# The gate product of both layers as wide matmuls over two banks by turns

## The chip, the cores and the metric

The kernel runs on one core of a Trainium2 chip. The metric is the device time of one execution in microseconds (us); lower is better. Engines work side by side and are tied by semaphores: PE (TensorE, matrix products), ACT (ScalarE), DVE (VectorE), POOL (GpSimd) and SP, which here issues the transfers of the weights.

## The reference, cut to what matters

Four layers of a network over 256 tokens of width 1024, all in fp32. The first two are other blocks (gated linear attention, stick-breaking attention, both with an MLP) and are not touched. The change is at the end of each of the last two layers:

```
for i in range(DEPTH):                                 # DEPTH = 2
    ...
    h = h + gated_conv_ffn(rms_norm(h, ffn_norm_w[i]), ...)
    gate = jax.nn.sigmoid(rms_norm(h, ple_norm_w[i]) @ w_ple_gate[i])   # 1024 x 1024
    h = h + gate * (p[i] @ w_ple_proj[i])                              # 256 x 1024
return rms_norm(h, final_norm_w)
```

The kernel multiplies by the norm's weight first, takes the product, and applies the one factor per token (the inverse root of the mean square, `rs1`) to the product.

## The kernel before, in words

**Precision and operands.** Every fp32 operand is split into a high and a low part, and a product is high·high + high·low + low·high. Activations lie with the feature on the partitions; `xs` holds for each of 8 feature tiles k the high tokens (`xhi`, 256 columns) and right beside them the low tokens (`xlo`, 256 columns).

**Weight stream.** All weights come as 208 chunks of 128x2048, in the order of use. SP loads chunk c into one of six buffers (`raw`), ACT makes its high part (`split_hi`, the cast of L283), DVE its low part (`split_lo`, the subtraction of L291). There are three buffers for each part, so both wait until chunk c-3 has been used (`chunk_used`), and PE waits for the low part (`lo_made`). A gate product is four chunks, C_GATE[L] to C_GATE[L]+3; chunk j gives 256 output features (two tiles t). Below they are called chunk 0 to 3, the next two (the projection, and the first of the next layer) chunk 4 and 5.

**Two ways to multiply a chunk.** `gemm` (L299 to L301) issues for each of 16 (k, t) three matmuls of 256 columns, all into the same half bank, so that PSUM bank b holds the finished sum for both tiles. `wide_gemm` (L390, L392) issues two: the low weight with the high tokens (256 columns) and the high weight with high and low tokens together (512 columns). It needs two whole banks, b for tile 0 and b+1 for tile 1. In each, columns 0 to 255 (`main_half`) hold two of the terms and columns 256 to 511 (`cross_half`) the third, so that someone has to add the halves. The MLPs and the gated FFN just ahead of the gate product are made so: ACT copies the cross half to SBUF (L1136, L1140), DVE adds the main half to it (L1643, L1668).

**The gate stage before.** PE: `gemm` for chunk j into bank j, j = 0 to 3, no bank used twice; after chunk 1 it sums the squares over the partitions (`squares_sum`, L515) into bank 3, which chunk 3 overwrites later, once `rs_made` says that ACT has read it. Then the projection into `acc` (`ple_projection`). ACT in program order: cast of chunk 2, squares, cast of chunk 3, logarithm and exponential for `rs1` (L981, L982), and then for j = 0 to 3: the cast of chunk j+3 (j = 1 and 2 only), and the sigmoid of output j (L1428) once DVE has scaled it (`z_scaled`). DVE in program order: the subtractions of chunks 1 and 2, the sum of squares (L1548 to L1550), and then for j = 0 to 3: the subtraction of chunk j+3 (j < 3), and the scaling of output j out of PSUM (L2007). After that the products with the projection (L2011), their addition to h (L1864) and, in the first of the two layers, the low part of the next activations (L1541). Every engine takes its instructions strictly in this written order.

Of the kernel before, what the change touches and what calls it, by code (L numbers as in the profile page):

```python
# [6 lines left out]
S = 256  # L7
# [10 lines left out]
LN_EPS, RMS_EPS = 1e-5, 1e-6  # L18
# [16 lines left out]
C_GATE = [c + 3 * N_FF for c in C_FFN]  # L35
# [19 lines left out]
def build_program(nc, xT, xtok, lnp, wstream, wa1, wa2, wf, fbias, pT, params, consts, decay, out):  # L55
    f32, f32r, i32 = mybir.dt.float32, mybir.dt.float32r, mybir.dt.int32
    ALU, ACT = mybir.AluOpType, mybir.ActivationFunctionType
    ctx = ExitStack()
    with ctx:
        def sb(name, shape, dt=f32):  # L60
            return ctx.enter_context(nc.sbuf_tensor(name, shape, dt))

        def sem(name):
            return ctx.enter_context(nc.semaphore(name))
# [11 lines left out]
        kT = sb("kT", [128, NT, S])  # L76
# [39 lines left out]
        def flat(t):  # L116
            return t[:, :, :].rearrange("p t s -> p (t s)")

        yf, sqf, qf, kf, gf, hf = (flat(t) for t in (y, sq, qT, kT, gT, hT))
        wa2_sb = sqf[:, 1536:2048]  # L120
        rs = misc[:, 2048:3072]
        rs1 = misc[:, 2048:2304]
        dec = misc[:, 0:2048].rearrange("p (h s) -> p h s", h=RET_H)

        def wide(ap, n):

            return ap.unsqueeze(1).to_broadcast([ap.shape[0], n, ap.shape[1]])

        def pair(t, j):
            return t[:, 2 * j:2 * j + 2, :]  # L130

        def two(ap):
            return ap.rearrange("p (t s) -> p t s", t=2)


        acc = ctx.enter_context(nc.psum_tensor("acc", [128, NT, S], f32))
        ring = ctx.enter_context(nc.psum_tensor("ring", [128, 4, 512], f32))

        def bank(i):
            return ring[:, i, :]  # L140
# [11 lines left out]
        chunk_used = sem("chunk_used")  # L152
# [21 lines left out]
        z_scaled, gelu_scaled = sem("z_scaled"), sem("gelu_scaled")  # L174
# [10 lines left out]
        signs_made = sem("signs_made")  # L185
        s_z, s_abs, s_ln, s_sp, s_hi, s_L, s_lw, s_w, s_wm, s_o = (sem("sb_" + n) for n in ("z", "abs", "ln", "sp", "hi", "L", "lw", "w", "wm", "o"))
        wf_in = sem("wf_in")
        f_part, f_copied = sem("fox_part"), sem("fox_copied")
        f_log, f_logit, f_ln, f_cum, f_z, f_mx, f_e, f_p, f_td, f_tc, f_o = (
            sem("fox_" + n) for n in ("log", "logit", "lnf", "cum", "z", "mx", "e", "p", "td", "tc", "o"))  # L190
# [79 lines left out]
        def cross_half(b):  # L270

            return ring[:, b:b + 2, 256:512]

        def main_half(b):
            return ring[:, b:b + 2, 0:256]

        def split_hi(act, c, m=0, per=RAW):
            if c >= N_CHUNKS:
                return
            act.wait_ge(raw_in[c % RAW], m * (16 * per // RAW) + 16 * (c // RAW + 1))  # L280
            if c >= SPLIT:
                act.wait_ge(chunk_used, m * per + (c - SPLIT + 1))
            act.copy(whi[:, c % SPLIT, :], raw[:, c % RAW, :]).then_inc(hi_made, 1)  # L283

        def split_lo(dve, c, m=0, per=RAW):
            if c >= N_CHUNKS:
                return
            dve.wait_ge(hi_made, m * per + (c + 1))
            if c >= SPLIT:
                dve.wait_ge(chunk_used, m * per + (c - SPLIT + 1))  # L290
            dve.tensor_tensor(wlo[:, c % SPLIT, :], raw[:, c % RAW, :], whi[:, c % SPLIT, :].bitcast(f32),  # L291
                              ALU.subtract).then_inc(lo_made, 1)
# [3 lines left out]
        def _(pe):  # L296
            def three(o, l1, l2, r1, r2, start, stop, **kw):

                pe.matmul(o, l1, r1, start=start, stop=False, **kw)  # L299
                pe.matmul(o, l1, r2, start=False, stop=False, **kw)  # L300
                return pe.matmul(o, l2, r1, start=False, stop=stop, **kw)  # L301

            def gemm(c, b, x_need=None, m=0, turned=False, between=None):


                pe.wait_ge(lo_made, m * RAW + (c + 1))
                wh, wl = whi[:, c % SPLIT, :], wlo[:, c % SPLIT, :]
                outs = [bank(b)[:, t * 256:t * 256 + 256] for t in range(2)]
                if x_need is not None:

                    for k in range(NT):
                        if turned and k % 4 == 0:
                            pe.wait_ge(x_made, 4 * x_need + k // 2 + 2)
                        if not turned and k % 2 == 0:
                            pe.wait_ge(x_made, 4 * x_need + k // 2 + 1)
                        for t in range(2):
                            w = slice(k * 256 + t * 128, k * 256 + t * 128 + 128)
                            mm = three(outs[t], wh[:, w], wl[:, w], xhi[:, k, :], xlo[:, k, :], k == 0 and t == 0,
                                       k == NT - 1, skip_group_check=True)
                    mm.then_inc(chunk_used, 1)  # L320
                    return
                for t in range(2):
                    if t and between is not None:
                        between()
                    for k in range(NT):
                        w = slice(k * 256 + t * 128, k * 256 + t * 128 + 128)
                        mm = three(outs[t], wh[:, w], wl[:, w], xhi[:, k, :], xlo[:, k, :], k == 0, k == NT - 1)
                mm.then_inc(chunk_used, 1)
# [183 lines left out]
            def squares_sum(n, o):  # L512

                pe.wait_ge(sq_summed, n + 1)
                pe.matmul(o, ones, sq[:, 0, :], start=True, stop=True).then_inc(var_done, 1)  # L515

            def ple_projection(c, L):

                pe.wait_ge(lo_made, c + 1)
                pe.wait_ge(p_lo, L + 1)  # L520
                for j in range(4):
                    pe.wait_ge(y_made, 4 * (2 + 3 * L) + j + 1)
                    for k in range(2):
                        for t in (2 * j, 2 * j + 1):
                            w = slice(k * D + t * 128, k * D + t * 128 + 128)
                            mm = three(acc[:, t, :], whi[:, c % SPLIT, w], wlo[:, c % SPLIT, w], hhi[:, 2, k, :],
                                       hlo[:, 2, k, :], k == 0 and t % 2 == 0, k == 1, skip_group_check=True)
                    mm.then_inc(*((proj_done, 1) if j < 3 else (chunk_used, 1)))
# [299 lines left out]
            for L in range(DEPTH):  # L828
                X = 6 + 4 * L
# [112 lines left out]
                for j in range(4):  # L942
                    if j == 3:
                        pe.wait_ge(rs_made, 3 * L + 3)
                    gemm(C_GATE[L] + j, j, X + 3 if j == 0 else None)
                    if j == 1:
                        squares_sum(3 * L + 2, bank(3)[:, 0:S])
                ple_projection(C_PROJ[L], L)
            for t in range(NT):
                pe.wait_ge(sq_made, 4 * 6 + (t // 2 + 1 if t < 6 else t - 2))  # L950
# [5 lines left out]
        def _(act):  # L956
# [22 lines left out]
            def power(r, psum, scale, eps):  # L979

                own.sync(act.activation(r, psum, ACT.Ln, bias=eps_col[eps], scale=scale))  # L981
                return act.activation(r, r, ACT.Exp, scale=-0.5)  # L982

            def inverse_root(n, psum, eps):

                act.wait_ge(var_done, n + 1)
                power(rs1, psum, 1 / D, eps).then_inc(rs_made, 1)
# [91 lines left out]
            def mlp(n):  # L1079
                c0, free, h0 = C_MLP[n], FREE[f"mlp{n}"], N_UP * n  # L1080

                def crossed(c, i, m=0):
                    act.wait_ge(chunk_used, m * 12 + (c + 1))
                    act.copy(pair(qT, i % 3), cross_half(2 * (i % 2))).then_inc(hid_cross, 1)  # L1084
# [26 lines left out]
                def last_crossed(t):  # L1111
                    act.wait_ge(*((chunk_used, cu + 1) if t else (up_half, n + 1)))
                    act.copy(qT[:, 2 * s + t, :], cross_half(2 * (i % 2))[:, t, :]).then_inc(hid_cross if t else half_cross, 1)
# [210 lines left out]
            for L in range(DEPTH):  # L1324
                X = 6 + 4 * L
# [93 lines left out]
                split_hi(act, C_GATE[L] + AHEAD)  # L1419
                squares_of_h(3 * L + 2)  # L1420
                split_hi(act, C_GATE[L] + 1 + AHEAD)
                inverse_root(3 * L + 2, bank(3)[:, 0:S], RMS_EPS)
                for j in range(4):
                    if 1 <= j < 3:
                        split_hi(act, C_GATE[L] + j + 1 + AHEAD)
                    act.wait_ge(z_scaled, 4 * L + j + 1)
                    z = kf[:, j * 512:j * 512 + 512]
                    act.activation(z, z, ACT.Sigmoid).then_inc(sig_made, 1)  # L1428
# [12 lines left out]
        def _(dve):  # L1441
# [424 lines left out]
            for L in range(DEPTH):  # L1866
                X = 6 + 4 * L
# [133 lines left out]
                for j in range(4):  # L2001
                    if j < 3:
                        split_lo(dve, C_GATE[L] + j + 1 + AHEAD)
                    if j == 0:
                        dve.wait_ge(rs_made, 3 * L + 3)
                    dve.wait_ge(chunk_used, C_GATE[L] + j + 1)
                    dve.tensor_tensor(pair(kT, j), two(bank(j)), wide(rs1, 2), ALU.mult).then_inc(z_scaled, 1)  # L2007
                for j in range(4):
                    dve.wait_ge(*((proj_done, 3 * L + j + 1) if j < 3 else (chunk_used, C_PROJ[L] + 1)))
                    dve.wait_ge(sig_made, 4 * L + j + 1)  # L2010
# [181 lines left out]
```

## Time and the profile before

| | us |
|---|---|
| median of three runs | 1316.61 (1316.28 to 1316.97) |
| the profiled execution, its time | 1316.21 |
| the profiled execution, span from first to last instruction | 1314.5 |
| busy in the span: PE / DVE / ACT | 1297.4 / 927.3 / 671.2 |

A busy PE here is one whose matmuls overlap with their neighbours: a matmul of 256 columns is shown as 0.28 us long while the next starts 0.12 us after it. So the distance from start to start is what a matmul takes of PE's time. All times of rows below are from the start of the span. The gate stage of the first layer (L = 0) begins at 929.14 us, that of the second (L = 1) at 1275.18 us.

### The profile page before, as it was taken

To read this page: it belongs to the slowest core of one execution; us is meant where nothing else is said; L and a number is where in the kernel's file an instruction comes from. 1 tells how busy PE (TensorE), PEld (TensorE's weight loads), DVE (VectorE), ACT (ScalarE), POOL (GpSimd) and SP (SyncE) were. 2 spreads that over 40 slices of the span, in tenths; PEclk is the share of its full clock that TensorE was granted. 3 is DMA by queue.
4 is the path that set the end of the run, shared out by engine and by line. 5 is a ranking of instruction groups with operands and counts; after the bars stand their busy time and mean duration, and the time that the engine had idled before them with its cause. 6 is when DMAs were issued, how large, how long until landed. Compare 5 with 4: busy or idle time off the path is not lost.

```text
span 1314.5 us, 21057 instructions
## 1 busy us (share of the span) xinstructions
PE 1297.4 (99%) x8368; PEld 1155.8 (88%) x8368; DVE 927.3 (71%) x1125; ACT 671.2 (51%) x767; POOL 45.8 (3%) x69
## 2 busy tenths in 40 slices
PE   9999999999999999999999999999999999999998
PEld 8898888887998888887998989999999888999997
DVE  4748655567566766558667787777796769877776
ACT  6645444445565444445444654444655546444454
POOL 0000000000133000001100000000020000000000
PEclk9999999999999999999999999999999999999999
DMA  9634655554433555554554355445545534545520
GB/s 378 263 119 172 245 192 192 191 192 160 161 129 129 217 186 186 186 189 139 186 177 145 129 192 191 179 177 186 192 141 190 191 112 148 219 176 181 188 96 33
DMA packets 34401, 231.85 MB, mean 176 GB/s; under 512 B 4000, under 2 KB 4256, under 8 KB 7200
## 3 DMA queue, kind: packets, MB, share of 16 engines
q1 hardware_dynamic: 31104, 219.17, 46.0%
q10 hardware_dynamic: 3232, 11.76, 2.7%
q8 instruction: 47, 0.77, 0.2%
q14 instruction: 18, 0.15, 0.0%
HBM read 227.77 MB, written 1.05 MB: 174 GB/s over the span
## 4 chain that ended last, share of the span: by engine, by line
PE 85%; DVE 8%; ACT 4%; issue 2%; DMA 1%; DVEq 0%; ACTq 0%
PE ring L392 19%; PE ring L390 10%; PE ring L299 9%; PE ring L301 8%; PE ring L300 8%; PE acc L424 4%; PE acc L426 4%; PE acc L425 4%; PE acc L301 3%; PE acc L299 3%; PE acc L300 3%; DVE wlo L291 3%; ACT whi L283 1%; PE ring L424 1%; PE ring L426 1%
## 5 line engine op out<-in xcount | busy, mean ns | idle before, releaser
L291 DVE TENSOR_TENSOR wlo<-raw,whi 128x2048 fp32r<-128x2048 f32 x206 | 472.3, 2298 | 132.5 <-ACT whi L283 132.0
L283 ACT CAST whi<-raw 128x2048 fp32r<-128x2048 f32 x202 | 384.8, 1908 | 119.7 <-PE ring L301 62.6
L392 PE MATMUL ring<-xs,whi 128*128 128x512 f32 x1184 | 419.6, 398 | 0.0
L390 PE MATMUL ring<-xs,wlo 128*128 128x256 f32 x1184 | 333.4, 282 | 1.1 <-DVE wlo L291 1.1
L392 PEld LDWEIGHTS ring<-xs,whi 128*128 128x128 f32 x1184 | 222.4, 188 | 53.1
L299 PE MATMUL ring<-xs,whi 128*128 128x256 f32 x832 | 240.6, 289 | 1.9 <-DVE xs L1541 0.8
L300 PE MATMUL ring<-xs,whi 128*128 128x256 f32 x832 | 235.3, 283 | 0.0
L301 PE MATMUL ring<-xs,wlo 128*128 128x256 f32 x832 | 235.2, 283 | 0.0
L390 PEld LDWEIGHTS ring<-xs,wlo 128*128 128x128 f32 x1184 | 223.7, 189 | 3.3 <-DVE wlo L291 1.8
L299 PEld LDWEIGHTS ring<-xs,whi 128*128 128x128 f32 x832 | 159.2, 191 | 9.1 <-issue 5.5
L300 PEld LDWEIGHTS ring<-xs,whi 128*128 128x128 f32 x832 | 159.4, 192 | 0.6 <-issue 0.5
L301 PEld LDWEIGHTS ring<-xs,wlo 128*128 128x128 f32 x832 | 159.3, 192 | 0.0
L299 PE MATMUL acc<-hhi,whi 128*128 128x256 f32 x384 | 108.8, 283 | 0.0
L301 PE MATMUL acc<-hhi,wlo 128*128 128x256 f32 x384 | 108.6, 283 | 0.0
L300 PE MATMUL acc<-hlo,whi 128*128 128x256 f32 x384 | 108.6, 283 | 0.0
L424 PE MATMUL acc<-whi,hhi 128*128 128x512 f32 x256 | 100.1, 391 | 0.0
L426 PE MATMUL acc<-whi,hlo 128*128 128x512 f32 x256 | 99.8, 390 | 0.0
L425 PE MATMUL acc<-wlo,hhi 128*128 128x512 f32 x256 | 99.6, 389 | 0.0
L300 PEld LDWEIGHTS acc<-hlo,whi 128*128 128x128 f32 x384 | 73.5, 191 | 0.9
L299 PEld LDWEIGHTS acc<-hhi,whi 128*128 128x128 f32 x384 | 73.5, 191 | 0.4 <-issue 0.4
L301 PEld LDWEIGHTS acc<-hhi,wlo 128*128 128x128 f32 x384 | 73.5, 192 | 0.0
L1084 ACT COPY qT<-ring 128x512 f32<-128x512 f32 x30 | 17.6, 586 | 98.0 <-PE ring L392 95.8
(296 smaller groups left out, 1673.7 us busy)
## 6 DMA issues: line engine op xcount, KB each, us to landing
raw<-wstream SPq DMA_DIRECT2D x206, 1024.0 KB, 4.8
sq<-lnp ACTq DMA_DIRECT2D x3, 1024.0 KB, 4.9
raw<-wstream SPq DMA_DIRECT2D x4, 256.0 KB, 5.2
hT<-xT ACTq DMA_DIRECT2D x4, 256.0 KB, 5.5
raw<-wstream SPq DMA_DIRECT2D x2, 512.0 KB, 8.3
hT<-xtok ACTq DMA_DIRECT2D x1, 1024.0 KB, 18.3
misc<-decay ACTq DMA_DIRECT2D x1, 1024.0 KB, 4.7
kT<-lnp ACTq DMA_DIRECT2D x1, 1024.0 KB, 4.8
```

Source lines behind the costliest of these rows:

```text
L283: act.copy(whi[:, c % SPLIT, :], raw[:, c % RAW, :]).then_inc(hi_made, 1)
L291: dve.tensor_tensor(wlo[:, c % SPLIT, :], raw[:, c % RAW, :], whi[:, c % SPLIT, :].bitcast(f32), ALU.subtract).then_inc(lo_made, 1)
L299: pe.matmul(o, l1, r1, start=start, stop=False, **kw)
L300: pe.matmul(o, l1, r2, start=False, stop=False, **kw)
L301: return pe.matmul(o, l2, r1, start=False, stop=stop, **kw)
L390: pe.matmul(bank(b + t)[:, 0:256], wl[:, w], xhi[:, k, :], start=k == 0, stop=False, skip_group_check=True)
L392: mm = pe.matmul(bank(b + t), wh[:, w], xs[:, k, :, :].rearrange("p a s -> p (a s)"), start=False, stop=k == NT - 1, skip_group_check=True)
L424: pe.matmul(o, l1[:, k, at], wh[:, w], start=first and k == 0, stop=False, skip_group_check=True)
L425: pe.matmul(o, l1[:, k, at], wl[:, w], start=False, stop=False, skip_group_check=True)
L426: mm = pe.matmul(o, l2[:, k, at], wh[:, w], start=False, stop=last and k == 1, skip_group_check=True)
L1084: act.copy(pair(qT, i % 3), cross_half(2 * (i % 2))).then_inc(hid_cross, 1)
```

## The change

PE uses `wide_gemm` for the four gate chunks, into the bank pairs 0-1, 2-3, 0-1, 2-3. ACT copies the cross half of each into an SBUF buffer (`z_part`, two by turns), DVE adds it to the main half, writes the sum to `kT` (`z_sum`), and scales that in a second instruction, from SBUF. Chunks 2 and 3 wait on PE until the sum of the chunk two before has been taken. The squares are summed into `acc` tile 7 in place of bank 3.

```diff
+        def z_part(j):
+            return two(gf[:, (j % 2) * 512:(j % 2) * 512 + 512])
@@ tensor
                 for j in range(4):
                     if j == 3:
                         pe.wait_ge(rs_made, 3 * L + 3)
-                    gemm(C_GATE[L] + j, j, X + 3 if j == 0 else None)
+                    if j >= 2:
+                        pe.wait_ge(z_sum, 4 * L + j - 1)
+                    wide_gemm(C_GATE[L] + j, 2 * (j % 2), X + 3 if j == 0 else None)
                     if j == 1:
-                        squares_sum(3 * L + 2, bank(3)[:, 0:S])
+                        squares_sum(3 * L + 2, acc[:, 7, :])
@@ scalar
                 split_hi(act, C_GATE[L] + 1 + AHEAD)
-                inverse_root(3 * L + 2, bank(3)[:, 0:S], RMS_EPS)
+                def z_crossed(j):
+                    act.wait_ge(chunk_used, C_GATE[L] + j + 1)
+                    act.copy(z_part(j), cross_half(2 * (j % 2))).then_inc(z_cross, 1)
+                z_crossed(0)
+                inverse_root(3 * L + 2, acc[:, 7, :], RMS_EPS)
                 for j in range(4):
                     if 1 <= j < 3:
                         split_hi(act, C_GATE[L] + j + 1 + AHEAD)
+                    if j < 3:
+                        z_crossed(j + 1)
                     act.wait_ge(z_scaled, 4 * L + j + 1)
                     z = kf[:, j * 512:j * 512 + 512]
                     act.activation(z, z, ACT.Sigmoid).then_inc(sig_made, 1)
@@ vector
                     if j < 3:
                         split_lo(dve, C_GATE[L] + j + 1 + AHEAD)
+                    dve.wait_ge(z_cross, 4 * L + j + 1)
+                    dve.tensor_tensor(pair(kT, j), main_half(2 * (j % 2)), z_part(j), ALU.add).then_inc(z_sum, 1)
                     if j == 0:
                         dve.wait_ge(rs_made, 3 * L + 3)
-                    dve.wait_ge(chunk_used, C_GATE[L] + j + 1)
-                    dve.tensor_tensor(pair(kT, j), two(bank(j)), wide(rs1, 2), ALU.mult).then_inc(z_scaled, 1)
+                    dve.wait_ge(z_sum, 4 * L + j + 1)
+                    dve.tensor_tensor(pair(kT, j), pair(kT, j), wide(rs1, 2), ALU.mult).then_inc(z_scaled, 1)
```

## Rows read from the trace of the kernel before

**Rows 1.** The page: busy time of the engines, and PE's granted clock in 40 slices.
```profile
PE 1297.4 (99%) x8368; PEld 1155.8 (88%) x8368; DVE 927.3 (71%) x1125; ACT 671.2 (51%) x767; POOL 45.8 (3%) x69
...
PEclk9999999999999999999999999999999999999999
```
**Rows 2.** PE in order of time (start us, us, engine, line), from FFN to next layer.
```profile
906.31 0.28 PE L390 MATMUL ring<-xs,wlo 128*128 128x256 f32 x1
...
917.62 0.28 PE L299 MATMUL acc<-hhi,whi 128*128 128x256 f32 x1
...
929.14 0.28 PE L299 MATMUL ring<-xs,whi 128*128 128x256 f32 x1
...
940.67 0.60 PE L515 MATMUL ring<-sq,cst 128*128 128x256 f32 x2
940.92 0.47 PE L299 MATMUL ring<-xs,whi 128*128 128x256 f32 x1
...
952.61 0.28 PE L299 MATMUL acc<-hhi,whi 128*128 128x256 f32 x1
...
960.48 0.39 PE L299 MATMUL ring<-xs,whi 128*128 128x256 f32 x1 [0.35 <-DVE xs L1541]
960.70 0.28 PE L300 MATMUL ring<-xs,whi 128*128 128x256 f32 x1
```
**Rows 3.** The chain that ended last (start us, us, what), in and behind the first gate stage.
```profile
951.39 1.46 DVE wlo L291
...
959.55 0.87 DVE xs L1541 x2
```
**Rows 4.** DVE in order of time, gate stage of the first layer.
```profile
939.43 2.28 DVE L291 TENSOR_TENSOR wlo<-raw,whi 128x2048 fp32r<-128x2048 f32 x1
942.27 0.69 DVE L2007 TENSOR_TENSOR kT<-ring,misc 128x512 f32<-128x512 f32 x1 [0.55 <-ACT misc L982]
946.00 2.29 DVE L291 TENSOR_TENSOR wlo<-raw,whi 128x2048 fp32r<-128x2048 f32 x1 [3.04 <-ACT whi L283]
948.21 0.68 DVE L2007 TENSOR_TENSOR kT<-ring,misc 128x512 f32<-128x512 f32 x1
...
953.60 1.28 DVE L2007 TENSOR_TENSOR kT<-ring,misc 128x512 f32<-128x512 f32 x2
954.80 0.68 DVE L2011 TENSOR_TENSOR kT<-kT,acc 128x512 f32<-128x512 f32 x1
955.51 0.69 DVE L1864 TENSOR_TENSOR hT<-hT,kT 128x512 f32<-128x512 f32 x1
956.12 0.68 DVE L2011 TENSOR_TENSOR kT<-kT,acc 128x512 f32<-128x512 f32 x1
```
**Rows 5.** ACT in order of time, gate stage of the first layer.
```profile
942.25 1.28 ACT L1428 ACT_TABLE_LOAD   x1
943.55 0.63 ACT L1428 ACTIVATE kT<-kT 128x512 f32<-128x512 f32 x1
944.09 1.89 ACT L283 CAST whi<-raw 128x2048 fp32r<-128x2048 f32 x1
```
**Rows 6.** ACT and DVE in order of time: one FFN chunk's halves joined and scaled.
```profile
912.16 0.59 ACT L1136 COPY y<-ring 128x512 f32<-128x512 f32 x1 [3.74 <-PE ring L392]
...
912.78 0.69 DVE L1643 TENSOR_TENSOR y<-ring,y 128x512 f32<-128x512 f32 x1 [2.04 <-ACT y L1136]
...
913.51 0.69 DVE L1646 TENSOR_TENSOR qT<-y,misc 128x512 f32<-128x512 f32 x1
```
**Rows 7.** PE in order of time, second layer: start of the projection.
```profile
1298.64 0.28 PE L299 MATMUL acc<-hhi,whi 128*128 128x256 f32 x1
```
**Rows 8.** DVE in order of time, second layer.
```profile
1300.28 0.69 DVE L2011 TENSOR_TENSOR kT<-kT,acc 128x512 f32<-128x512 f32 x1 [0.75 <-PE acc L301]
...
1304.60 0.69 DVE L2011 TENSOR_TENSOR kT<-kT,acc 128x512 f32<-128x512 f32 x1
```
**Rows 9.** Who PE waited for, whole span: us in total, times, longest.
```profile
PE ring L367 <- DVE y L1718: 1.3, 1, 1.3
```

More of the change, by code:

```diff
@@ L187, in build_program @@
         wf_in = sem("wf_in")
+        z_cross, z_sum = sem("z_cross"), sem("z_sum")
         f_part, f_copied = sem("fox_part"), sem("fox_copied")
```

## The prediction

> **What bounds the kernel now.** I read the page first. PE is busy 1297.4 of 1314.5 us, and DVE and ACT are far from full [rows 1]. So the span is PE's work, and a change pays by taking matmul time away or costs by making PE, or whoever hands to it at a seam, late. Next I read PE in order of time through the gate stage. From 929.14, chunks 0 and 1 run until 940.67, then the squares, then chunks 2 and 3 from 940.92 until the projection starts at 952.61, and nothing in it is a wait [rows 2]. Before the change PE never waits in this stage. That doesn't mean that only PE is tight there: the chain that ended last runs through DVE's and ACT's part of the stage [rows 3], because DVE then makes the activations for which PE waits in the next layer (0.35 us before 960.48, [rows 2]). So two lines run abreast: PE's, and the one of casts, subtractions, scalings and sigmoids, which ends in the products with the projection (954.80, [rows 4]). Both have to be carried through the change. The second layer repeats the first 346.03 us later (PE at 1298.64 against 952.61) [rows 2, 7], up to its end.
>
> **Part 1: the matmuls.** A chunk of `gemm` is 48 matmuls. From 929.14 to 940.67 there are two chunks, so one takes 5.765 us, 0.120 a matmul. A wide chunk has 32 matmuls; two of them in the FFN run from 906.31 to 917.62 without a gap, so one takes 5.655 us [rows 2]. The array streams the same 768 columns for each (k, t) either way, so only the cost of an instruction is saved: 0.11 us a chunk, 0.22 before the squares, 0.88 over eight chunks. That is all that the change can win, 0.07%.
>
> [...]
>
> **Part 2: the first bank wait.** Chunk 2 now goes into chunk 0's banks, and waits for the sum of output 0. PE is ready for it at 940.67 - 0.22 + 0.25 (the squares) = 940.70. ACT copies the cross half of chunk 0 right behind the cast of chunk 3, in a stretch in which it stood idle, so it isn't late. DVE is: the sum stands in its queue behind the subtraction of chunk 3, which starts at 939.43, because the subtractions of chunks 1 and 2 and the sum of squares fill DVE before it. This subtraction's successor starts 2.21 us after it (948.21 after 946.00) [rows 4], so the sum starts at 941.64. It is like L1643, which takes 0.69 [rows 6], so it ends at 942.33, and PE starts 0.06 later (960.42, where the activations of L1541 end, to 960.48, [rows 2, 3]), at 942.39. PE stands 1.69 us. Before, DVE scaled output 0 at 942.27 and nobody waited for it; the same lateness was free, since the banks weren't reused.
>
> **Part 3: the sigmoid of output 0 and the second bank wait.** The squares come 0.22 us earlier, so ACT is through with the exponential at about 942.03 instead of 942.25. Now the copy of chunk 1's cross half follows (0.59, [rows 6]), and only then the table load of the sigmoid: 942.03 + 0.61 = 942.64. The sigmoid starts 1.30 after the start of its table load [rows 5], at 943.94 against 943.55, 0.39 late; DVE's scaling is done by 943.05, so the table is the last to come. Behind the sigmoid in ACT's queue is the cast of chunk 4 (944.09, now 944.48), and behind that cast waits DVE's subtraction of chunk 4 (946.00, now 946.39). Only behind this stands the sum of output 1: 948.21 + 0.39 = 948.60, end 949.29. PE needs it for chunk 3. Chunk 2 started at 942.39 and runs 5.655, with 0.10 more because the first matmul after a stand is followed at 0.22 instead of 0.12 (960.48 to 960.70) [rows 2]; it is over at 948.15. PE starts chunk 3 at 949.35, and stands 1.20 us. The projection starts at 949.35 + 5.75 = 955.10 instead of 952.61, 2.49 late. Here the change's wait sits in a loop: chunk 3 waits for a sum that stands behind a subtraction that stands behind a cast that stands behind a sigmoid.
>
> **Part 4: the line through DVE, first layer.** Each output now costs DVE a sum and a scaling. The scaling waits for the sum's own semaphore, so it starts 0.71 after it (as 955.51 after 954.80); the next instruction without such a wait starts 0.61 later (956.12 after 955.51) [rows 4]. Scaling 1: 948.60 + 0.71 = 949.31, against 948.21, so 1.10 late. Sigmoid 1, the cast and the subtraction of chunk 5 hang on it and are 1.10 late too (there was no slack there, [rows 3]), and the sum of output 2 starts at 953.60 + 1.10 = 954.70. Its scaling 955.41. The sum of output 3 could start at 956.02; its copy starts when chunk 3's last matmul has ended, 955.10 + 0.16 = 955.26, and hands over 0.62 later (912.16 to 912.78, [rows 6]), at 955.9, just in time. Scaling 3 at 956.73, first product at 957.34 against 954.80: 2.54 late. From there the work is as before, all on DVE, and PE's next layer hangs on it [rows 2], so layer one gives 2.54.
>
> **Part 5: second layer.** The PE side is the same: first stand 1.69, second 1.20, projection at 1301.13 for 1298.64. There is no chunk 5, so DVE is free when chunk 3 ends at 1301.29. The copy and hand-over take 0.03 + 0.62, the sum starts at 1301.94, the scaling at 1302.65, the first product at 1303.26, against 1300.28: 2.98 late. But before, the products followed the projection, 1.44 apart (1300.28 to 1304.60 for three) [rows 8], while DVE alone needs 1.32 (954.80 to 956.12) [rows 4]. So it catches up 0.36: the fourth starts at 1303.26 + 3.96 = 1307.22 against 1304.60, 2.62 late. The projection's own last part allows 1307.09, so DVE decides by a hair. The final norm follows as before.
>
> **What costs nothing.** Moving the squares to `acc` tile 7: its last reader, the addition at L1864, is over before chunk 0 is half done. The eight copies on ACT, 0.59 each: the first and the last three fall where ACT waited for DVE or PE; the one of chunk 1 is priced above. The weight stream isn't touched, and its loads only get 2.5 us more time.
>
> **The sum.** 2.54 + 2.62 = 5.2 us. On the profiled execution that is 1316.21 + 5.2 = 1321.4 (span 1319.7); the median of the runs is 0.4 above that execution, so 1321.8, 0.39% slower.
>
> **The rivals.** *The second wait closes.* If ACT and DVE reached the sum of output 1 before PE asked (1.2 us earlier than I work out), only the first stand of 1.69 less the matmuls saved would be left, about 1.4 a layer on PE's line; the second layer's tail adds its 0.4 to 0.6. The DVE line must then be shorter too. That gives +3.2, 1319.8. The sigmoid table's 0.39 speaks against it, with the queue order. Chance 8 in 100. *PE doesn't stand* (the other side). Then the whole effect is the 0.88 of part 1, 1315.8, not slower. Its place is the sum of output 0: it decides from the point at which this sum ends by 940.64. It would have to stand ahead of the 2.21 us of the subtraction, and the written order forbids that. What is left is a trace whose distances mislead, or a seam elsewhere that swallows both delays. PE waits for DVE right behind the first layer's stage [rows 2], which speaks against slack there, and behind the second there is only the tail. Chance 6, of which 3 with one layer's delay swallowed (+2.6, 1319.2). *A table load more.* The copies stand between exponential and sigmoid and between sigmoids. If one asked for another table, each pair of switches would cost 1.28 to 2.6 us [rows 5] a layer, 1324 to 1327. The casts between the sigmoids bring no load now, and are the same operation. Chance 3. *PE's clock falls.* The granted clock is full in all slices [rows 1], past a wait of 1.3 us near the start [rows 9]. The new stands are 1.7 and 1.2 us, in one stage. [...] Chance 3. [...]
>
> **How the numbers follow.** My forecast has 80 in 100. What it can't know: the sum reading two banks with a stride (as L1643, which does just that), the restart after a stand (0 to 0.3 a stand, four of them), a wide chunk's time in this stage (between the FFN's 5.655 and `gemm`'s 5.765, up to +0.9), and which of two nearly equal lines ends last; together about -1.0 to +1.5. Range 1319.5 to 1323.6: it takes in the closed second wait and a small part of the table case. Changes under 0.2% (2.6 us) can hardly be told from none. Slower 0.91 (forecast, closed second wait, table, clock, less the part of these that ends under +2.6), the same 0.07, faster 0.02.
>
> **What would show it.** In the profile of the changed kernel: PE idle ahead of L390 by DVE's sum, twice a layer, about 1.7 and 1.2 us, four waits and some 5.8 us in all; L390 and L392 128 more each, L299 to L301 128 fewer each; the sigmoid's table load 0.39 later against the stage's start; first product at DVE 28.2 us after the stage's start (957.34 - 929.14), in the second layer 28.1; the clock still full. The prediction is wrong if PE shows no wait at chunk 3, or if the next layer's start takes back some of the first 2.5 us.

## The result and the profile after

The changed kernel takes 1321.42 us (median of 7 runs, 1320.78 to 1321.81) against 1316.71 (7 runs beside them): 1.0037 times as long, 95% interval 1.0028 to 1.0046. That is 4.7 us slower; 1321.8 was forecast, with a range of 1319.5 to 1323.6. The profiled execution has a span of 1319.7 us.

The page of the changed kernel, busy time, granted clock, and the two groups of the wide pair among the costliest:

```profile
PE 1298.0 (98%) x8240; PEld 1148.9 (87%) x8240; DVE 932.3 (71%) x1133; ACT 675.2 (51%) x775; POOL 45.7 (3%) x69
...
PEclk9999999999999999999999999999999999999999
...
L397 PE MATMUL ring<-xs,whi 128*128 128x512 f32 x1312 | 464.9, 397 | 0.0
L395 PE MATMUL ring<-xs,wlo 128*128 128x256 f32 x1312 | 370.0, 282 | 5.7 <-DVE kT L2020 2.4
```

PE's busy time is what it was [rows 1], and the span is 5.2 us longer: the loss is not work, it is standing. The granted clock is full in every slice, 0.999 of full speed over the execution, as in the kernel before, so that rival is out. The wide pair has 128 more each (1312 for 1184), and the idle time ahead of its first matmul is now 5.7 us, where it was 1.1. The same line of the page of the kernel before:

```profile
L390 PE MATMUL ring<-xs,wlo 128*128 128x256 f32 x1184 | 333.4, 282 | 1.1 <-DVE wlo L291 1.1
```

Who PE waited for in the changed kernel (us in total, times, longest). L395 is the first matmul of a wide pair, L2020 the new sum:

```profile
PE ring L395 <- DVE kT L2020: 2.4, 2, 1.2
PE ring L395 <- issue: 2.3, 2, 1.2
...
PE ring L372 <- DVE y L1733: 1.3, 1, 1.3
PE ring L395 <- DVE wlo L296: 1.1, 2, 0.5
```

Four new waits, two in each layer. The trace ties two of them to the sum, and calls the other two "issue", that is without a releaser that it can name; the order of time shows what they are. PE in the first gate stage, the lines that answer to [rows 2]:

```profile
934.98 0.39 PE L395 MATMUL ring<-xs,wlo 128*128 128x256 f32 x1
...
940.74 0.59 PE L520 MATMUL acc<-sq,cst 128*128 128x256 f32 x2
942.54 0.38 PE L395 MATMUL ring<-xs,wlo 128*128 128x256 f32 x1 [1.21 <-DVE kT L2020]
...
947.85 0.28 PE L395 MATMUL ring<-xs,wlo 128*128 128x256 f32 x1
949.53 0.36 PE L395 MATMUL ring<-xs,wlo 128*128 128x256 f32 x1 [1.17 <-issue]
```

And DVE beside it, the lines that answer to [rows 4]; L296 is the subtraction, L2020 the sum, L2024 the scaling, L2028 the product with the projection:

```profile
939.60 2.29 DVE L296 TENSOR_TENSOR wlo<-raw,whi 128x2048 fp32r<-128x2048 f32 x1
941.80 0.68 DVE L2020 TENSOR_TENSOR kT<-ring,gT 128x512 f32<-128x512 f32 x1
942.59 0.69 DVE L2024 TENSOR_TENSOR kT<-kT,misc 128x512 f32<-128x512 f32 x1
946.54 2.29 DVE L296 TENSOR_TENSOR wlo<-raw,whi 128x2048 fp32r<-128x2048 f32 x1 [3.26 <-ACT whi L288]
948.75 0.68 DVE L2020 TENSOR_TENSOR kT<-ring,gT 128x512 f32<-128x512 f32 x1
949.47 0.69 DVE L2024 TENSOR_TENSOR kT<-kT,misc 128x512 f32<-128x512 f32 x1
...
954.86 0.68 DVE L2020 TENSOR_TENSOR kT<-ring,gT 128x512 f32<-128x512 f32 x1
...
957.52 0.68 DVE L2028 TENSOR_TENSOR kT<-kT,acc 128x512 f32<-128x512 f32 x1
```

The first sum ends at 942.48, and PE resumes 0.06 later. The second ends at 949.43, and PE resumes 0.10 later: that "issue" is the same wait. Both sums stand right behind a subtraction of 2.3 us. The stage begins at 929.30 here, so DVE's first product comes 957.52 - 929.30 = 28.22 us into it, against 954.80 - 929.14 = 25.66 before [rows 2, 4]: 2.56 late.

### The profile page after: what moved, and what is told of

Its sections match the earlier page's. It is cut to its first block, busy times and chain, and to the rows that moved or that the text cites. A ratio compares the mean times of both kernels' runs of the same rounds, so it can differ in the third digit from the quotient of the medians.

```text
span 1319.7 us, 20819 instructions
## 1 busy us (share of the span) xinstructions
PE 1298.0 (98%) x8240; PEld 1148.9 (87%) x8240; DVE 932.3 (71%) x1133; ACT 675.2 (51%) x775; POOL 45.7 (3%) x69
## 4 chain that ended last, share of the span: by engine, by line
PE 84%; DVE 9%; ACT 4%; issue 2%; DMA 1%; DVEq 0%; ACTq 0%
PE ring L397 20%; PE ring L395 10%; PE ring L304 8%; PE ring L306 7%; PE ring L305 7%; PE acc L429 4%; PE acc L431 4%; PE acc L430 4%; PE acc L306 3%; PE acc L304 3%; PE acc L305 3%; DVE wlo L296 3%; ACT whi L288 2%; PE ring L429 1%; PE ring L431 1%
## 5 line engine op out<-in xcount | busy, mean ns | idle before, releaser
L296 DVE TENSOR_TENSOR wlo<-raw,whi 128x2048 fp32r<-128x2048 f32 x206 | 472.3, 2298 | 132.5 <-ACT whi L288 132.0
L397 PE MATMUL ring<-xs,whi 128*128 128x512 f32 x1312 | 464.9, 397 | 0.0
L395 PE MATMUL ring<-xs,wlo 128*128 128x256 f32 x1312 | 370.0, 282 | 5.7 <-DVE kT L2020 2.4
L397 PEld LDWEIGHTS ring<-xs,whi 128*128 128x128 f32 x1312 | 246.4, 188 | 58.4
L395 PEld LDWEIGHTS ring<-xs,wlo 128*128 128x128 f32 x1312 | 247.9, 189 | 9.9 <-DVE kT L2020 3.2
L304 PE MATMUL ring<-xs,whi 128*128 128x256 f32 x704 | 204.0, 290 | 1.9 <-DVE xs L1556 0.8
L305 PE MATMUL ring<-xs,whi 128*128 128x256 f32 x704 | 199.1, 283 | 0.0
L304 PEld LDWEIGHTS ring<-xs,whi 128*128 128x128 f32 x704 | 134.7, 191 | 9.0 <-issue 5.7
L305 PEld LDWEIGHTS ring<-xs,whi 128*128 128x128 f32 x704 | 134.8, 192 | 0.6 <-issue 0.5
```

The source lines that it names most:

```text
L395: pe.matmul(bank(b + t)[:, 0:256], wl[:, w], xhi[:, k, :], start=k == 0, stop=False, skip_group_check=True)
L397: mm = pe.matmul(bank(b + t), wh[:, w], xs[:, k, :, :].rearrange("p a s -> p (a s)"), start=False, stop=k == NT - 1, skip_group_check=True)
```

## The experiments

Every kernel was timed beside the kernel before. Runs of one kernel lie up to 2 us apart (the kernel before from 1315.59 to 1317.08, the free banks from 1317.98 to 1320.03), so beside the medians stand four distances in each trace, which leave out what happened ahead of the first gate stage. They are differences of starts in the order of time: from the start of the first gate stage (first matmul of chunk 0) to DVE's first product; from the same start to that of the second gate stage, which holds the whole effect on layer one; from the second stage's start to DVE's fourth product; and from there to the end of the span, which holds the effect on layer two. The second distance runs through the whole next layer and is less exact than the first: in the eight traces of the experiments it reads 0.1 to 0.2 more against before than the first product does, and what makes that isn't shown.

| kernel | us, median | ratio (95%) | 1st product, layer 1 | stage 1 to stage 2 | 4th product, layer 2 | stage 2 to end |
|---|---|---|---|---|---|---|
| before | 1316.71 | | 25.66 | 346.04 | 29.42 | 39.3 |
| changed | 1321.42 | 1.0037 (1.0028 to 1.0046) | 28.22 | 348.60 | 32.08 | 41.8 |
| free banks | 1319.07 | 1.0020 (1.0011 to 1.0029) | 28.23 | 348.74 | 29.31 | 39.1 |
| matmuls alone | 1316.35 | 0.9997 (0.9988 to 1.0006) | 25.54 | 346.15 | 29.13 | 39.1 |
| sums, narrow | 1319.42 | 1.0021 (1.0012 to 1.0030) | 28.31 | 348.84 | 29.60 | 39.3 |
| copy behind cast | 1320.50 | 1.0032 (1.0020 to 1.0045) | 27.74 | 348.28 | 31.61 | 41.3 |
| sums first | 1317.18 | 1.0005 (0.9996 to 1.0014) | 26.77 | 347.28 | 29.30 | 39.0 |
| best order | 1315.88 | 0.9997 (0.9988 to 1.0006) | 25.32 | 345.79 | 29.30 | 39.0 |
| best order again | 1315.48 | 0.9993 (0.9984 to 1.0002) | 25.33 | 345.84 | 29.08 | 38.7 |
| last chunk narrow | 1315.66 | 0.9993 (0.9984 to 1.0002) | 24.91 | 345.51 | 29.12 | 39.0 |

(The kernel before ran again beside each group: 1316.68 beside the free banks, the matmuls, the narrow sums and the sums first; 1316.10 beside the moved copy and the best order; 1316.39 beside the last two.)

The theory is the prediction's: two lines run abreast, PE's through the bank waits, and that of DVE and ACT through the sums, the late sigmoid and the subtractions; both are late by about the same. The chief rival is the plain reading of the profile after, that PE's stands are the cost.

**1. Free banks.** Chunks 2 and 3 go into the accumulator's four banks, which are empty then, and the projection into the ring. PE waits for the sums of outputs 0 and 1 only ahead of the projection.

```diff
-                    if j >= 2:
-                        pe.wait_ge(z_sum, 4 * L + j - 1)
-                    wide_gemm(C_GATE[L] + j, 2 * (j % 2), X + 3 if j == 0 else None)
+                    wide_gemm(C_GATE[L] + j, 2 * (j % 2), X + 3 if j == 0 else None, to=acc_bank if j >= 2 else bank)
...
+                pe.wait_ge(z_sum, 4 * L + 2)
                 ple_projection(C_PROJ[L], L)
...
-                    act.copy(z_part(j), cross_half(2 * (j % 2))).then_inc(z_cross, 1)
+                    act.copy(z_part(j), z_cross_half(j)).then_inc(z_cross, 1)
```

> The changed kernel without bank reuse: chunks 2 and 3 go into the four accumulator banks, the projection into the ring, so PE has no wait for a sum. Two-lines theory (PE's line and the DVE/ACT line are both late, about equally): PE's two stands per layer vanish, but DVE's first product in layer one stays 2.5 us late, because sums, scalings and the late sigmoid are still in its queue; only layer two, which ends on PE's projection, gets its delay back (about -0.3 against before). Time about +2.3 over before, 1319.0. Rival (the stands of PE are the whole cost): all of it comes back, 1315.8 to 1316.2. Rival (wide matmuls are slow here): nothing comes back, 1321.

Measured 1319.07. The largest of PE's waits in this kernel (L310 is `gemm`, L1562 the low part of its activations):

```profile
PE ring L310 <- DVE xs L1562: 3.6, 3, 2.8
```

PE in order of time, the longest of these three waits, at the start of the next layer:

```profile
960.40 0.35 PE L310 MATMUL ring<-xs,whi 128*128 128x256 f32 x1 [2.81 <-DVE xs L1562]
```

The stands inside the gate stage are gone: squares at 11.44 and projection at 23.18 us into the stage, 0.3 earlier than before. In layer one that buys nothing: the first product is where the changed kernel has it (28.23 to 28.22), and PE stands 2.81 us at the start of the next layer instead. In layer two, where the rest waits for the end of chunk 3 on PE, all comes back at the fourth product. So about half of the loss would stay if the banks were never reused, and the chief rival falls. In the profile after, PE's waits of 2.4 and 2.3 us add up to nearly the whole loss, and still they alone don't make it in layer one.

**2. The matmuls alone.** The layout of 1, without copies and sums. DVE scales the main half, so the third term of the product is left out.

```diff
-                    dve.wait_ge(z_cross, 4 * L + j + 1)
-                    dve.tensor_tensor(pair(kT, j), z_main_half(j), z_part(j), ALU.add).then_inc(z_sum, 1)
-                    dve.wait_ge(z_sum, 4 * L + j + 1)
-                    dve.tensor_tensor(pair(kT, j), pair(kT, j), wide(rs1, 2), ALU.mult).then_inc(z_scaled, 1)
+                    dve.wait_ge(chunk_used, C_GATE[L] + j + 1)
+                    dve.tensor_tensor(pair(kT, j), z_main_half(j), wide(rs1, 2), ALU.mult).then_inc(z_scaled, 1)
```

> The wide matmuls alone, in the same banks as e1, with no copy and no sum: DVE scales the main half only, so the third term of the product is left out. Two-lines theory: two chunks take 11.44 us as in the changed kernel (chunk 1 waits for its low part), the squares come 0.1 early; layer one gains 0.1 (DVE's line decides), layer two 0.4 (PE's line): 1316.2. Rival (a wide chunk in this stage costs more than gemm's): above 1316.7. Rival (all 0.88 of the saving is on the path): 1315.8.

Measured 1316.35, not to be told from no change. The first product is 0.12 earlier, the fourth of layer two 0.29. The wide form isn't slower here; it saves a tenth of a microsecond a chunk in layer two and two tenths in layer one (see the last section), and most of that isn't on the path.

**3. The sums alone.** The narrow matmuls into four banks, with the copies and sums where the change has them; copy and sum both read the finished bank, so the gate's input is doubled.

```diff
-                    if j >= 2:
-                        pe.wait_ge(z_sum, 4 * L + j - 1)
-                    wide_gemm(C_GATE[L] + j, 2 * (j % 2), X + 3 if j == 0 else None)
+                    gemm(C_GATE[L] + j, j, X + 3 if j == 0 else None)
...
-                    act.copy(z_part(j), cross_half(2 * (j % 2))).then_inc(z_cross, 1)
+                    act.copy(z_part(j), two(bank(j))).then_inc(z_cross, 1)
...
-                    dve.tensor_tensor(pair(kT, j), main_half(2 * (j % 2)), z_part(j), ALU.add).then_inc(z_sum, 1)
+                    dve.tensor_tensor(pair(kT, j), two(bank(j)), z_part(j), ALU.add).then_inc(z_sum, 1)
```

> The other half of the change alone: gemm's narrow matmuls into four banks as before, but with ACT's four copies and DVE's four sums in the places where the change has them (copy and sum read the finished bank, so the gate's input is doubled). PE waits for no sum. Two-lines theory: layer one about +2.75 at the first product (sigmoid 0.58 late with no matmul time saved, then a sum ahead of scaling 1, a sum ahead of scaling 3), layer two about +0.2: together +2.9, 1319.6. Rival (only PE's stands cost): within 0.3 of before.

Measured 1319.42. First product 28.31, 2.65 late; fourth product of layer two 0.18 late. Without one wait of PE in the gate stage and without wide matmuls, eight copies and eight sums cost 2.7 us in these places of two queues (6 shows that it is the places). Together with 1 this says where the loss sits: layer one's half in DVE's and ACT's line, layer two's half in PE's bank waits. In layer one PE's line is late beside it, but by less: its projection starts 25.96 us into the changed kernel's stage, and the first product follows a projection by 1.64 where nothing else holds it (1298.64 to 1300.28, [rows 7, 8]). By this estimate PE alone would hold it to 27.60, 1.9 late and not 2.56. No run keeps PE's waits and frees DVE's line, so this part isn't tested by itself.

**4. One copy moved.** ACT copies chunk 1's cross half behind the cast of chunk 4 instead of ahead of the sigmoid's table load.

```diff
                     if 1 <= j < 3:
                         split_hi(act, C_GATE[L] + j + 1 + AHEAD)
-                    if j < 3:
+                    if j == 1:
+                        z_crossed(1)
+                    if 1 <= j < 3:
                         z_crossed(j + 1)
```

> The changed kernel with one of ACT's copies moved: that of chunk 1 from ahead of the sigmoid's table load to behind the cast of chunk 4. Nothing else. Two-lines theory: it takes the copy's 0.58 us out of the way of sigmoid 0, the cast and the subtraction of chunk 4, the sum of output 1 and so of both lines, in both layers: -0.6 each, 1320.2; PE's second stand shrinks from 1.2 to 0.6, the first stays. Rival (the second stand hangs on something other than that queue): no change, 1321.4.

Measured 1320.50. First product 0.48 earlier than in the changed kernel, fourth product of layer two 0.47 earlier, and the second stands together 1.3 us where they were 2.3, while the first keep their 2.4. The distances alone show this: the second stage starts 0.32 earlier and the tail is 0.5 shorter, but against the kernel before beside it (1316.10) the time is 4.4 longer, which can't be told from the changed kernel's 4.7. The term was 0.1 too large. The changed kernel's ACT (L989 the exponential, L1432 the copy, L1443 the sigmoid) shows why:

```profile
941.88 0.42 ACT L989 ACTIVATE misc<-misc 128x256 f32<-128x256 f32 x1
942.20 0.57 ACT L1432 COPY gT<-ring 128x512 f32<-128x512 f32 x1
942.78 1.28 ACT L1443 ACT_TABLE_LOAD   x1
944.08 0.63 ACT L1443 ACTIVATE kT<-kT 128x512 f32<-128x512 f32 x1
```

The copy starts 0.10 before the exponential has ended, so it costs the table load 0.48 and not 0.58. The whole chain of copy, table, sigmoid, cast, subtraction, sum and PE moved by that 0.48: one copy on ACT decides when PE starts chunk 3.

**5. The sums first.** DVE's order changed only: the sum of output 0 ahead of the subtraction of chunk 3, each next sum behind the scaling before it. The banks are reused as in the change.

```diff
+                summed(0)
                 for j in range(4):
                     if j < 3:
                         split_lo(dve, C_GATE[L] + j + 1 + AHEAD)
-                    dve.wait_ge(z_cross, 4 * L + j + 1)
-                    dve.tensor_tensor(pair(kT, j), main_half(2 * (j % 2)), z_part(j), ALU.add).then_inc(z_sum, 1)
...
                     dve.tensor_tensor(pair(kT, j), pair(kT, j), wide(rs1, 2), ALU.mult).then_inc(z_scaled, 1)
+                    if j < 3:
+                        summed(j + 1)
```

> The changed kernel with DVE's order changed: the sum of output 0 ahead of the subtraction of chunk 3, and each next sum directly behind the scaling before it, ahead of the next subtraction. Banks are reused as in the change. Two-lines theory: both stands of PE go, because only the order made them; the late sigmoid (0.37) stays, the sum and scaling of output 3 stay behind the last subtraction: first product of layer one 1.1 late, layer two -0.3, together +0.8, 1317.5. Rival (reusing two banks by turns is itself the cost): stands remain, 1320 to 1321.

Measured 1317.18. No stand is left in the gate stage (projection 22.96 and 23.18 us in), with the same two bank pairs by turns. The first product is 1.11 late, as expected, though the median can't be told from before. So reusing two pairs of banks costs nothing in itself; the place of the sum in DVE's queue did.

**6. The best order, twice.** Besides, on ACT the cast of chunk 4 ahead of sigmoid 0 and that of chunk 5 ahead of sigmoid 1, on DVE sum and scaling of output 2 ahead of the subtraction of chunk 5.

```diff
-                    if 1 <= j < 3:
-                        split_hi(act, C_GATE[L] + j + 1 + AHEAD)
                     if j < 3:
                         z_crossed(j + 1)
+                    if j < 2:
+                        split_hi(act, C_GATE[L] + j + 2 + AHEAD)
                     act.wait_ge(z_scaled, 4 * L + j + 1)
...
+                    if j in (0, 1, 3):
+                        split_lo(dve, C_GATE[L] + (2 if j == 3 else j) + 1 + AHEAD)
...
+                    if j == 3:
+                        summed(3)
...
+                    if j < 2:
+                        summed(j + 1)
```

> The sums first, and besides on ACT the cast of chunk 4 ahead of sigmoid 0 and that of chunk 5 ahead of sigmoid 1, on DVE sum and scaling of output 2 ahead of the subtraction of chunk 5. All parts of the change are kept. Two-lines theory: nothing is late any more; layer one ends 0.4 earlier than before, bound by chunk 3's end, its copy, sum and scaling; layer two 0.3 earlier: 1316.0. Rival (the sums cannot be hidden, DVE is too full): 1317 or more.

> The best order once more, beside the kernel above on the same chip: -0.5 against before by the distances of its first trace, 1316.1 where before is 1316.7.

Measured 1315.88 and 1315.48, beside 1316.10 and 1316.39. DVE in the first gate stage of the first of them (L2019 the sum, L2030 the scaling, L2036 the product; the stage starts at 929.48):

```profile
939.77 0.68 DVE L2019 TENSOR_TENSOR kT<-ring,gT 128x512 f32<-128x512 f32 x1
940.37 2.28 DVE L296 TENSOR_TENSOR wlo<-raw,whi 128x2048 fp32r<-128x2048 f32 x1
942.57 0.68 DVE L2030 TENSOR_TENSOR kT<-kT,misc 128x512 f32<-128x512 f32 x1
943.17 0.69 DVE L2019 TENSOR_TENSOR kT<-ring,gT 128x512 f32<-128x512 f32 x1
944.78 2.29 DVE L296 TENSOR_TENSOR wlo<-raw,whi 128x2048 fp32r<-128x2048 f32 x1 [0.92 <-ACT whi L288]
...
953.47 0.69 DVE L2019 TENSOR_TENSOR kT<-ring,gT 128x512 f32<-128x512 f32 x1 [1.56 <-ACT gT L1432]
954.19 0.69 DVE L2030 TENSOR_TENSOR kT<-kT,misc 128x512 f32<-128x512 f32 x1
954.80 0.68 DVE L2036 TENSOR_TENSOR kT<-kT,acc 128x512 f32<-128x512 f32 x1
```

All of the change's work is in it, and the whole loss of 4.7 us is gone. What is left in front of the first product is the copy of chunk 3 and its sum and scaling.

**7. The last chunk narrow.** As 6, with chunk 3 by `gemm` into bank 2 and scaled straight out of it.

```diff
-                    wide_gemm(C_GATE[L] + j, 2 * (j % 2), X + 3 if j == 0 else None)
+                    if j == 3:
+                        gemm(C_GATE[L] + 3, 2)
+                    else:
+                        wide_gemm(C_GATE[L] + j, 2 * (j % 2), X + 3 if j == 0 else None)
...
+                    if j == 3:
+                        dve.wait_ge(chunk_used, C_GATE[L] + 4)
+                        dve.tensor_tensor(pair(kT, j), two(bank(2)), wide(rs1, 2), ALU.mult).then_inc(z_scaled, 1)
+                        continue
```

> The best order, with chunk 3 multiplied by gemm's narrow matmuls into one bank and scaled straight out of it, so that only chunks 0 to 2 are wide and have a sum. Two-lines theory: in the best order the first product (25.32 us after the stage's start) is held by chunk 3's copy, sum and scaling alone; without copy and sum it comes when the projection's first part is done, at 24.9 against 25.66 before, so layer one gains 0.75 and layer two, which ends on PE's projection, 0.2: together -0.9 to -1.0, 1315.7 where before is 1316.7. Rival (the best order is at PE's bound already, and chunk 3's 0.1 us of matmuls is lost): same as or 0.1 above the best order's -0.5.

Measured 1315.66. The first product comes at 24.91, where the projection allows it, 0.75 earlier than before. But the second stage starts only 0.53 earlier, and the median can't be told from that of 6. The step is shown in the trace; that it is worth more than 6 is not.

## Why the prediction was right

**Size.** 5.2 us were forecast on the span; the profiled spans differ by 5.2 (1319.7 to 1314.5) and the stage distances by 2.56 + 2.5 = 5.1. The medians differ by 4.7, so the forecast was 0.5 high, inside the interval (3.7 to 6.1 us). That the spans agree to the tenth is in part luck: 0.16 of the difference lies ahead of the first gate stage (929.30 to 929.14), and the profiled execution of the kernel before, 1316.21, is quicker than all seven runs beside the changed kernel.

**Part 1, the matmuls:** right for the wide pair, mis-sized for what it brings before the squares. Two chunks were to take 11.31 us; they take 11.44, so 0.09 is saved and not 0.22. The sum left out that chunk 1 has to wait for its own low part: that subtraction starts at 932.64, ends at 934.93, and PE starts chunk 1 at 934.98, 5.68 us after chunk 0. The wait itself costs 0.03, and the slow restart of the first matmul (the next starts 0.22 after it, at 935.20) another 0.10. Before, the low part came 0.14 ahead of need (932.48 + 2.28 against 934.90) and didn't show. A gain on PE ran into the next engine's date within one chunk. Part 3 begins with the opposite slip: the copy was to cost the sigmoid 0.61 and costs 0.48 (experiment 4). The two slips cancel, and that is luck; the sigmoid is 0.37 late where 0.39 was forecast. Experiment 2 puts the saving at 0.10 us a chunk (chunks 2 and 3 with the squares 11.74 us in layer two, 11.94 before), 6 ns for each matmul saved; that this is the cost of an instruction was the author's reading, the runs show the difference alone. In layer one the same stretch takes 11.53, at a quicker pace that the last section shows.

**Part 2, the first stand:** right. PE was to stand from 940.70 to 942.39 of a stage starting at 929.14, that is to 13.25 us; measured 13.24. The stand itself is 1.55 instead of 1.69 (940.99 to 942.54), for the same reason as above. Experiment 5 shows that DVE's order is its cause.

**Part 3, the second stand:** right in mechanism and a little small: chunk 3 was to start at 20.21, measured 20.23; PE stands 1.33 us by the starts (948.20, one pair after 947.85, to 949.53) where 1.20 were forecast, since chunk 2 took 5.66 (942.54 to 948.20) and not 5.755. By the starts the four stands of both layers add up to 5.7 us, for 5.8 forecast; the list of waits shows 4.7 for the same, since it counts from the end that the trace shows for the matmul before (947.97 + 0.39 = 948.36 for the second stand, so 1.17 and not 1.33). Experiment 4 shows that what ACT does ahead of the table load and the cast sets the end of this stand.

**Part 4, DVE's line in layer one:** forecast 2.54, measured 2.56. Experiments 1 and 3 show that this line is late by itself, with PE's waits taken away. This was the step that could not have been read off the waits of the profile after.

**Part 5, layer two:** the fourth product was to be 2.62 late, measured 2.66. Experiment 1 shows that here the bank waits are the cause: free banks give all of it back. They act by the end of chunk 3, behind which the copy, the sum and DVE's products follow; that DVE and not the projection ends last, by a hair, is as forecast (32.08, where the projection would allow 25.96 + 1.64 + 4.32 = 31.92). The final norm takes some 0.17 of the delay back (39.3 to 41.8 us from the stage's start to the end), which was not foreseen. The traces show when this happens: the end comes 9.9 us after the fourth product where the products start 1.44 apart (before, matmuls alone, last chunk narrow), and 9.7 to 9.8 where they start 1.32 apart (all the others). Why the norm is shorter then isn't shown.

**The rivals.** That the second wait closes, that PE doesn't stand, that a table is loaded once more, that the clock falls: none came. ACT has the two table loads of before in the first stage (1.28 us each, at 931.83 and 942.78; before at 931.66 and 942.25), and PE's four stands of 1.6 and 1.2 to 1.3 us didn't move the granted clock: it is 1.00 within each of them and through the chunks behind them. The lowest mean granted clock of any execution is 0.996, so no run shows what a fall would cost.

## What to carry to other kernels

A change that makes an engine's buffer come round sooner has its price in the queue of whoever frees the buffer: look up which instruction stands in front of the freeing one, and how long it is (here a subtraction of 2.29 us ahead of the sum). When two lines run abreast into a seam, carry the change through both; the list of PE's waits showed 4.7 us on one line and nothing of the 2.57 us by which the other was late without them, and removing these waits (free banks) brought back half, 2.3 of 4.7 us. Before giving up such a change, write the order anew: the short instructions that release another engine ahead of the long ones that only prepare later work turned +4.7 us into nothing to be told from zero, and the gain that was to be had, 0.88 us by the forecast, is so small that no order tried here can be told from the kernel before by its time.

## What the runs showed of the hardware

A pair of wide matmuls (256 and 512 columns) takes 0.353 us in the FFN (11.31 us for 32 pairs from 906.31 in the kernel before) and 0.354 at the start of the changed kernel's gate stage (14 pairs from 929.66 to 934.61 take 4.95 us), but 0.347 through chunk 2 of its first layer (14 pairs from 942.99 to 947.85 take 4.86 us). In layer two of the same trace it is 0.353 (14 pairs from 1291.60 to 1296.54 take 4.94 us). The granted clock is 1.00 in all four stretches. The same two speeds show without any stand: chunks 2 and 3 with the squares take 11.53 us in layer one of the matmuls alone and 11.74 in layer two. What decides between them stays open; it is worth 0.2 us in two chunks, as much as the wide form saves in two chunks in layer two.
